# Attention stage of a hybrid decoder layer: on TensorE the products with the values of a unit are put ahead of the turn of the next unit's probabilities

## The reference, cut to what matters

```
for blk in range(seq // FOX_BLOCK):                  # 8 blocks of 128 queries
    start, end = blk * FOX_BLOCK, (blk + 1) * FOX_BLOCK
    scores = einsum('bhqd,bhkd->bhqk', q[start:end], k[:end]) * scale
    scores = scores + cum[start:end, None] - cum[None, :end]
    scores = where(mask, scores, -inf)
    probs = softmax(scores, axis=-1)
    outs.append(einsum('bhqk,bhkd->bhqd', probs, v[:end]))
```

## Time and profile before

| | us |
|---|---|
| median of 3 runs | 2629.93 (2625.29 to 2634.12) |
| the profiled execution | 2629.0 |
| its span | 2627.3 |
| units of stage 3 on PE | 495 to 718 of the span |
| PE busy, all stages | 2271.8 (86%) |
| DVE busy | 1580.2 (60%) |
| ACT busy | 1279.7 (49%) |

### The profile page before, as it was taken

One profiled execution on the slowest core, in us unless ns is written; L12 is line 12 of the kernel. 1 busy time (PEld: TensorE's weight loads), 2 busy tenths in 40 slices (PEclk: granted clock), 3 DMA queues, 4 the chain that ended last, 5 costly groups with the idle time before them and its releaser, 6 DMA issues. The chain is left out here.

```text
span 2627.3 us, 38117 instructions
## 1 busy us (share of the span) xinstructions
PE 2271.8 (86%) x12235; PEld 1945.5 (74%) x12236; DVE 1580.2 (60%) x1703; ACT 1279.7 (49%) x1692; POOL 471.8 (18%) x610
## 2 busy tenths in 40 slices
PE   4899948599889169999999999999999999999960
PEld 3788837488878068787888788788777887788850
DVE  4320048464632536668766776665888767876646
ACT  4121123353532135657665665665766656666540
POOL 1430015231200521111111021011121110111104
PEclk9999979575989579999999999999999999999985
DMA  4123130322242356879976897787999968989759
GB/s 138 57 92 112 49 88 25 77 58 91 79 163 104 109 188 225 290 254 336 330 239 225 273 342 237 261 268 235 326 356 342 337 222 275 357 278 305 242 188 367
DMA packets 453455, 560.96 MB, mean 214 GB/s; under 512 B 62804, under 2 KB 342357, under 8 KB 453397
## 3 DMA queue, kind: packets, MB, share of 16 engines
q1 hardware_dynamic: 440373, 517.46, 60.1%
q0 software_dynamic: 13024, 42.75, 4.4%
HBM read 504.73 MB, written 55.35 MB: 213 GB/s over the span
## 5 line engine op out<-in xcount | busy, mean ns | idle before, releaser
L1511 DVE TENSOR_TENSOR VL<-RAW,VH 128x2048 fp32r<-128x2048 f32 x389 | 887.7, 2290 | 309.2 <-ACT VH L1506 309.1
L1506 ACT ACTIVATE VH<-RAW 128x2048 fp32r<-128x2048 f32 x390 | 726.0, 1908 | 54.7 <-DMA RAW<-in_expert_w_gate_up 46.6
L1883 PE MATMUL banks<-T,VH 128*128 128x384 f32 x1920 | 547.2, 359 | 1.7 <-DVE T L1735 1.7
L1885 PE MATMUL banks<-T,VL 128*128 128x192 f32 x1680 | 421.5, 251 | 0.0
L1883 PEld LDWEIGHTS banks<-T,VH 128*128 128x128 f32 x1920 | 354.0, 189 | 2.8 <-issue 1.9
L1885 PEld LDWEIGHTS banks<-T,VL 128*128 128x128 f32 x1680 | 321.7, 191 | 0.6
L165 PE MATMUL banks<-VH,A 128*128 128x512 f32 (+1 forms) x752 | 301.1, 400 | 0.0
L167 PE MATMUL banks<-VH,A 128*128 128x512 f32 (+1 forms) x752 | 300.4, 400 | 0.0
L166 PE MATMUL banks<-VL,A 128*128 128x512 f32 (+1 forms) x752 | 299.9, 399 | 0.0
L167 PE MATMUL banks<-VH,T 128*128 128x512 f32 x544 | 212.2, 390 | 0.0
L166 PE MATMUL banks<-VL,T 128*128 128x512 f32 x544 | 212.2, 390 | 0.0
(11 more groups left out here) (310 smaller groups left out, 3822.5 us busy)
## 6 DMA issues: line engine op xcount, KB each, us to landing
RAW<-in_expert_w_gate_up SPq DMA_DIRECT2D x264, 1024.0 KB, 7.6
RAW<-in_expert_w_down SPq DMA_DIRECT2D x130, 1024.0 KB, 7.6
dY<-yb SPq DMA_DIRECT2D x98, 128.0 KB, 7.3
RAW<-in_w_in SPq DMA_DIRECT2D x6, 2048.0 KB, 8.6
dY<-zeros SPq DMA_DIRECT2D x17, 512.0 KB, 5.9
dY<-yb SPq DMA_DIRECT2D x32, 256.0 KB, 7.6
xin<-in_x SPq DMA_DIRECT2D x8, 512.0 KB, 4.3
qks<-dK SPq DMA_DIRECT2D x16, 256.0 KB, 3.8
```

The source lines that it names most:

```text
L1506: act.activation(VH[:, i, ks], RAW[:, i, ks], ACT.Copy).then_inc(s_hi, 1)
L1511: dve.tensor_tensor(VL[:, i, ks], RAW[:, i, ks], VH[:, i, ks].bitcast(f32), ALU.subtract).then_inc(s_w, 1)
L1883: last = pe.matmul(o[:, 0:2 * NW].rearrange("p (a n) -> p a n", a=2), VH[:, c % 3, k, col], T2[:, :, k], start=k == 0, stop=k == KT - 1)
L1885: pe.matmul(o[:, 0:NW], VL[:, c % 3, k, col], T2[:, 0, k], start=False, stop=False)
```

## The change

`values(u)` moves from the end of the loop's body to a place between `scores(u + 2)` and `turn(u + 1)`:

```diff
                 for u in range(NU):
                     if u + 2 < NU:
                         scores(u + 2)
+                    values(u)
                     if u + 1 < NU:
                         turn(u + 1)
                     if u % H in PREP and u // H + 1 < TT:
                         prepare(PREP[u % H][0], u // H + 1, PREP[u % H][1])
-                    values(u)
```

## The result

The changed kernel is slower: 2672.8 us median (2666.26 to 2681.15, 4 runs) against 2629.41 us for the kernel before, a ratio of 1.0166 (95% interval 1.0127 to 1.0205), or 43 us more. In a second set of runs, beside new runs of the kernel before, it was 1.0152 (1.0110 to 1.0194). The forecast was 2647 us with a range up to 2666: the sign was right, the size (18 us) less than half of what came.

What follows compares the result with a forecast made beforehand. The prediction took the attention stage to be bound by PE, busy 202.8 of 223 us. New waits, less exponent waits they replace, summed to 18.2 us on the profiled 2629.0, giving 2647 us, range 2632 to 2666.

Steps and rivals of the forecast that it cites:

- the new loop: In the attention units: turn, high part, low part, values, next turn; PE waits where turn and scores (and prepare) are shorter.
- rival 3: At the turns: values fill PE's 11.3 us of waits for the exponent, giving 2618 us; chance 0.07.
- L: Time from a turn's start to the PE work its low part releases: 2.16 us at full clock, 2.58 at half.
- the two last values: At the stage's end: both sets of values wait 1.37 us; 2.3 us in all after subtracting one exponent wait.
- the forecast's sum of 18.2: Over the attention stage: all new waits, less exponent waits they replace, add 18.2 us, with bounds 13 to 24.
- the rule: For each unit at full clock: wait is 2.16 us less turn and scores; 18 to 24 us at full clock everywhere.
- by clock and size, with this execution's clock: Over the 36 units without prepare: waits were sized by tile size and the profiled run's clock, such as 1.7 us at t = 7.
- rival 1: At 560 to 590 us: longer waits keep that stretch at half clock, 15 us more, 2662 us; chance 0.18.
- Rival 2: At 590 to 648 us: full clock comes back sooner, taking off 16 us, giving 2631 us; chance 0.15.

Runs made afterwards that it cites:

- e1: The kernel before, with the values put ahead of the next turn only at t = 7 (8 units): 2632.98 us, ratio 0.9999.
- e9: The changed kernel plus repeated products ahead of scores in units without prepare and in the prepares' waits at t >= 4: 2615.55 us, ratio 0.9940.
- e11: The kernel before plus 5 repeated products in each prepare's wait at t >= 4 and one or two ahead of scores for t < 4: 2601.09 us, ratio 0.9875.
- e2: The kernel before, with the values put ahead of the next turn only for t = 0 to 3 (32 units): 2652.2 us, ratio 1.0075.
- e4: The changed kernel plus 1 to 3 repeated products ahead of the scores of units without prepare: 2641.85 us, ratio 1.0033.
- e5: The kernel before plus 5 repeated products in each prepare's wait at t >= 4: 2609.43 us, ratio 0.9915.
- e3: The kernel before, with the values put ahead of the next turn only for t = 4 to 6 (24 units): 2639.52 us, ratio 1.0037.
- e6: The kernel before, with the values moved between turn and prepare for t >= 4, no product added: 2608.81 us, ratio 0.9910.
- e7: The kernel before, with values between turn and prepare, and on ACT the next exponent ahead of the prepare's high part, for t >= 4: 2598.03 us, ratio 0.9873.

## Why the prediction was right or wrong

**What bounds the stage, and the new loop: right, with one misreading.** Values wait in front of line 1055 for DVE line 939, in 28 places for 15.6 us (35 to 40 and near 20 forecast; in part because more units of t = 4 and 5 ran at half clock, where the wait is short or none). The prepares wait as before, the waits for the exponent shrink. The forecast added the rows of PE and PEld for these: 20 turns waited 7.8 us, not 29 turns 11.3. Its 0.39 us each holds by luck, since 7.8 / 20 and 3.5 / 9 are both 0.39, so the sum keeps its terms; the price of rival 3 should have been 7.8 us at most.

**L and the sizes of the waits: right, a little large.** The 2.16 us were 2.16 for the values at t = 4 and 2.07 at t = 7, so the pace there is 3.88 us, not 3.95; the two last values start 2.07 us after their turns, that is 2.07 - 0.79 = 1.28 us later than they could (1.37 forecast), of which 0.98 us shows as idle time, since the last transposes are still running at first. t = 4 came as written at full clock (3.27) and at half (4.68, 0.07 more than before, 0.11 forecast). In e1, at an unchanged clock, t = 7 with the end cost 3.3 us in the trace (4.0 forecast). At nearly equal clock, in e9 and e11, all waits are about 17 us (8 to 26); the forecast's sum of 18.2 was for a different mix of clocks, which is why the two may only be compared through the rule. In the changed kernel itself, mostly at half clock, PE's idle time grew by only 6.4 us.

**The step that failed: "by clock and size, with this execution's clock".** The sum took the half-clock stretches of the earlier trace rows as given. They grew from 111 to 177 us, and PE was busy 32 us longer with the same products. This was called rival 1, with a chance of 0.18 and a price of 15 us, to be reached if the stretch from 560 to 590 were lost. The mechanism is right and the price was too low: the whole was 43 us where rival 1 had 33. It was worked out for one stretch alone; the trace shows four changes, less full clock before 575, the short full-clock stretch, the 88 us behind it, and a new half-clock one in t = 6. The argument against it, that at t = 6 and 7 the new waits are small, does not help: t = 6 lost the clock in e2's trace too, where it has no new waits, so new waits in t = 6 itself are not needed for that. The swing of the clock between its levels, which the Trainium skill describes for short idle times between groups of matmuls (TensorE: Matmul & The Clock Gate, "A second HAM failure mode: psum-queue depth-cycling"), was cited and discounted; e4, e5, e9 and e11, which take idle time away and get the clock back, agree with it.

**Rival 2 (the clock comes back sooner) and rival 3 (the values fill the wait for the exponent): not seen.** The argument against rival 3 held: the low part is ready later than the exponent, as values wait 15.6 us after the change and turns 1.8.

**Open.** When exactly the clock falls or rises is not explained. e2 and e3 took different courses in different runs, and a single trace is only one course. For t = 0 to 3 the kernel of e3 has the order of before, yet its trace (first line) was at full clock in t = 2 where the trace of the kernel before (second line) was at half, though PE had no idle time there at all:

```profile
534.40:559.60 25.20, 23.61 (x180) 20.71 (x178) 20.77 (x37) 17.36 (x43) 10.14 (x11) 1.00 0.32 74
```

```profile
534.40:559.60 25.20, 25.20 (x113) 24.62 (x113) 14.31 (x25) 11.15 (x29) 7.44 (x8) 0.50 0.23 53
```

So the absence of idle time did not bring full clock back there. That less idle time of PE in the stage goes with less half clock is shown, by added work (e4, e5, e9, e11) and by work that was only moved (e6, e7); how much of it, and where, sets off a change is not.

## What to carry to other kernels

Where PE is nearly full and the granted clock in the profile changes between its levels, count a wait twice: its own length, and the time at half clock that it may bring on. Here waits worth about 17 us at equal clock came with a loss of 43, of which 32 were the same products taking longer. Read the clock row of the stage first, and before trusting a sum made at the old clock, price the case that every full-clock stretch next to new idle time is lost. Where PE must wait, look for work that can stand there: moving the values into the wait of the prepares gave 1%, and even repeated products that compute nothing gave as much.

## What the runs showed of the hardware that was not expected

Useless work made both orders faster. Five repeated products in each of 12 waits, which left the pace of a unit as it was (4.49 us at t = 4 before and after), took 22 us off the kernel before (ratio 0.9915), as the half clock in the stage went from 111 to 65 us. In the changed kernel the two fills took off 57 us (2672.8 to 2615.55), as it went from 177 to 25 us.
